# Output projections computed in two turns over the tokens, in a two-block transformer kernel on one Trainium2 core

## The reference, cut to what matters

```python
def rms_norm_2(x, g):
    y = xf * rsqrt(mean(xf * xf, axis=-1) + EPS);  return y * g

# layer i of 2; hx and hc hold 1024 features of 512 and 256 tokens
hx = rms_norm_2(x, g_pre) * (1.0 + scale_x) + shift_x
hc = rms_norm_2(ctx, g_pre) * (1.0 + scale_c) + shift_c
z = h @ w_in                        # queries, latents, gates ...
m = sum over 3 branches of sigmoid(g) * ((y * silu(z)) @ w_branch)
out = m @ w_o                       # the output projection, 1024 x 1024
x   = x   + gate_x * rms_norm_2(out_x, g_post)
ctx = ctx + gate_c * rms_norm_2(out_c, g_post)     # layer 0 only
```

## Time and profile before

| | |
|---|---|
| median of three runs | 2616.11 us |
| the profiled execution's own time | 2613.08 us |
| its span in the profile | 2611.3 us |
| TensorE busy with matmuls | 2467.3 us, 94% |
| VectorE, ScalarE, GpSimd busy | 45%, 35%, 20% |
| mean granted TensorE clock | 0.968 of full |

### The profile page before, as it was taken

How to read it: one execution, slowest core, us unless ns; L and a number is a source line. 1 busy time by engine, 2 the same in 40 slices (tenths; PEclk the granted TensorE clock), 3 DMA queues, 4 the chain that set the end, 5 groups by cost and what they waited for, 6 DMA issues and landing times.

```text
span 2611.3 us, 34190 instructions
## 1 busy us (share of the span) xinstructions
PE 2467.3 (94%) x14039; PEld 1976.7 (76%) x14039; DVE 1180.7 (45%) x1849; ACT 915.4 (35%) x1576; POOL 532.1 (20%) x381
## 2 busy tenths in 40 slices
PE   6887888899999999999999999999989999999998
PEld 5665666677788876778877888888866677878876
DVE  3735545454433444562257313323457633733432
ACT  3324543342222234552246211123335533632223
POOL 3003222140200211231004110012433210321023
PEclk8987899999999989999999999999989999999998
DMA  5231133245443311001210122113121023023232
GB/s 166 65 115 33 33 119 124 74 153 162 142 133 97 109 59 41 25 17 49 81 41 2 49 73 65 57 57 106 50 85 33 25 65 113 9 65 111 75 109 85
DMA packets 195740, 200.60 MB, mean 77 GB/s; under 512 B 15832, under 2 KB 189624, under 8 KB 195330
## 3 DMA queue, kind: packets, MB, share of 16 engines
q1 hardware_dynamic: 191106, 178.23, 21.8%
q10 hardware_dynamic: 4480, 20.19, 2.0%
HBM read 187.92 MB, written 10.49 MB: 76 GB/s over the span
## 4 chain that ended last, share of the span: by engine, by line
PE 85%; DVE 6%; ACT 4%; POOL 2%; issue 2%; DMA 1%; ACTq 0%; POOLq 0%; SPq 0%; DVEq 0%
PE PS L719 20%; PE PS L720 20%; PE PS L722 20%; PE PS L837 5%; PE PS L867 4%; PE PS L851 3%; DVE WL L1888 1%; PE PS L798 1%; ACT WH L1317 1%; PE PS L910 1%; PE PS L937 1%; PE PS L923 1%; PE PS L966 1%; POOL RB L2638 1%; PE PS L775 1%
## 5 line engine op out<-in xcount | busy, mean ns | idle before, releaser
L719 PE MATMUL PS<-HH,WH 128*128 128x512 f32 (+3 forms) x2048 | 757.0, 370 | 9.7 <-DVE WL L1888 4.8
L720 PE MATMUL PS<-HL,WH 128*128 128x512 f32 (+3 forms) x2048 | 726.9, 367 | 0.0
L722 PE MATMUL PS<-HH,WL 128*128 128x512 f32 (+3 forms) x2048 | 659.2, 365 | 0.0
L1888 DVE TENSOR_TENSOR WL<-WB,WH 128x2048 fp32r<-128x2048 f32 (+3 forms) x158 | 324.0, 2051 | 666.4 <-ACT WH L1317 658.5
L719 PEld LDWEIGHTS PS<-HH,WH 128*128 128x128 f32 (+1 forms) x2048 | 384.1, 188 | 117.0 <-issue 13.9
L720 PEld LDWEIGHTS PS<-HL,WH 128*128 128x128 f32 (+1 forms) x2048 | 384.0, 187 | 71.6 <-issue 2.9
L1317 ACT ACTIVATE WH<-WB 128x2048 fp32r<-128x2048 f32 (+3 forms) x158 | 265.1, 1678 | 340.1 <-PE PS L722 270.7
L722 PEld LDWEIGHTS PS<-HH,WL 128*128 128x128 f32 (+1 forms) x2048 | 348.1, 188 | 44.6
L2663 POOL TENSOR_SCALAR SA<-SA,ST 128x768 f32<-128x768 f32 (+4 forms) x80 | 142.0, 1776 | 534.8 <-DVE ST L1969 534.8
L2638 POOL TENSOR_TENSOR RB<-RB,SA 128x512 f32<-128x512 f32 (+2 forms) x65 | 89.3, 1374 | 391.2 <-ACT SA L1336 330.0
L1957 DVE TENSOR_REDUCE ST<-PS 128x1 f32<-128x768 f32 (+4 forms) x176 | 130.0, 739 | 71.0 <-PE PS L837 57.5
(11 more groups left out here) (366 smaller groups left out, 3716.7 us busy)
## 6 DMA issues: line engine op xcount, KB each, us to landing
WB<-in_w_in_dram SPq DMA_DIRECT2D x61, 1024.0 KB, 5.2
WB<-in_w_ff_dram SPq DMA_DIRECT2D x32, 1024.0 KB, 5.4
WB<-in_w_mod_dram SPq DMA_DIRECT2D x24, 1024.0 KB, 5.3
WB<-in_w_branch_dram SPq DMA_DIRECT2D x24, 512.0 KB, 3.5
WB<-in_w_o_dram SPq DMA_DIRECT2D x8, 1024.0 KB, 5.2
WB<-in_w_in_dram SPq DMA_DIRECT2D x14, 512.0 KB, 5.1
XTc<-xd ACTq DMA_DIRECT2D x2, 3072.0 KB, 10.0
WB<-in_cmp_w_dram SPq DMA_DIRECT2D x4, 1024.0 KB, 5.4
```

The source lines that it names most:

```text
L719: pe.matmul(D[0:m, d + o:d + o + w], h, xh[:, o:o + w], start=first, stop=False)
L720: pe.matmul(D[0:m, d + o:d + o + w], h, xl[:, o:o + w], start=False, stop=False)
L722: t = pe.matmul(D[0:m, d + o:d + o + w], lo, xh[:, o:o + w], start=False, stop=last)
L1888: dve.tensor_tensor(b.of(WL[s % NH]), b.of(WB[b.n % NW]), b.of(WH[s % NH]).bitcast(F32), ALU.subtract).then_inc(*done("wl", s))
```

## The change

The projections of both layers are cut by tokens. In layer 0 the first turn is `x` (512 columns) and the second, late turn `ctx` (256); in layer 1 they are the two halves of `x`, 256 columns each. The late turn takes the output tiles in the order 4, 5, 6, 7, 0, 1, 2, 3: the first four find their weights still in `WH` and `WL`, the others need blocks 0 and 1 loaded and split again, two more blocks for each layer. Its eight tiles lie side by side in two PSUM buffers. The sums, the roots, the spread and the making of layer 1's inputs are written once for each side; those of the first turn stand ahead of the late turn's evacuation on ScalarE, VectorE and GpSimd, and between the late turn's tiles on TensorE. `ql1` starts on the `x` half alone; the `ctx` half is made behind `ql1`'s first two tiles, and `kvl1` does its `x` columns before its `ctx` columns. In layer 1 the first half's transposes stand between the late tiles. `XTc`, `OT`, `ot`, `AC` and `QS` get other places in memory.

```diff
--- before.py
+++ after.py
@@ weight_blocks
-        cut(f"o{l}", I["w_o_2"][l])
+        for u in range(6):
+            i = u if u < 4 else u - 4
+            name = f"o{l}" if u < 4 else f"o{l}c"
+            add(Block(name, i, 8, 256, True, lambda w, s=I["w_o_2"][l][:, 256 * i:256 * i + 256]: [
+                (w[:, :, :], s.rearrange("(k p) c -> p k c", p=128))], ("lin", f"o{l}" if u < 2 else f"o{l}c", 2 * i + 1)))
@@ build
+        TURNS = {0: {"x": (0, NX, 0), "c": (NX, NC, 1)}, 1: {"x": (0, 256, 0), "c": (256, 256, 0)}}
+        LATE = (4, 5, 6, 7, 0, 1, 2, 3)
@@ tensor_program: ql1 and kvl1
+                    ps.order = [2, 3]
+                    linear_pair("ql1", hx(NT), nt, queries, lambda k: [next_low("x", k)])
+                    out_sums("c")
+                    tile = linear("ql1", hx(NT), nt, queries, parts=[1], pace=4)
+                    next(tile)
+                    next(tile)
+                    spread_columns("o0c", NC)
+                    spread_columns("h1c", NC)
+                    drain(tile)
+                    linear_sides("kvl1", 2, NT, lambda j: [("kvr_a" if j % 2 else "kvr_d", 1, j)],
+                                 lambda s, k: [next_low("c", k)] if s else [])
@@ tensor_program: the end of a layer
+                def out_sums(side):
+                    o, n, _ = TURNS[0][side]
+                    N, H, Q = f"o0{side}", f"h1{side}", f"oo{side}"
+                    ps.order = [2, 3] if side == "x" else [0, 1]
+                    D = slot(("norm", N), ("on", 0, side, 7))
+                    pe.wait_ge(*at("nadd", N, 7))
+                    add_columns(D, 0, n, RB[rb[N]], True, True).then_inc(*done("nsum", N))
+                    E = slot(("norm", H), ("hn", H, 7))
+                    pe.wait_ge(*at("cross", side, 7, "sum"))
+                    add_columns(E, 6, n, AC[0][:, o:o + n], True, True)
+                    pe.wait_ge(*at("nadd", Q, 7))
+                    add_columns(E, 0, n, AC[1][:, o:o + n], False, True).then_inc(*done("nsum", H))
+                    ps.order = [0, 1] if side == "x" else [2, 3]
+                def between(j):
+                    if l == 0:
+                        if j == 5:
+                            out_sums("x")
+                        elif j == 6:
+                            spread_columns("o0x", NX)
+                            spread_columns("h1x", NX)
+                    elif j == 4:
+                        last_sums("x")
+                    elif j == 5:
+                        spread_columns("o1x", 256)
+                    elif j in (1, 3):
+                        turn_out("x", j // 2)
-                drain(linear(f"o{l}", hx(nt), nt, lambda j: [("ot_a", l, j)], parts=[1, 2, 3]))
+                drain(linear(f"o{l}", half("x"), TURNS[l]["x"][1], lambda j: [("ot_a", l, "x", j)], parts=[1, 2, 3]))
+                for i, j in enumerate(LATE):
+                    b = of[f"o{l}" if i < 4 else f"o{l}c"][j // 2]
+                    if i % 4 == 0:
+                        ps.order = [i // 4]
+                        D = slot(("late", l, i // 4), ("ot_a", l, "c", LATE[i + 3]))
...
+                    t.then_inc(*done("lin", f"o{l}c", j))
+                    between(j)
@@ scalar_program: the end of a layer
+                def early_steps():
+                    if l == 0:
+                        yield
+                        out_roots("x")
+                        late_weights(1)
+                        for f, _ in enumerate(next_high("x")):
+                            if f in (1, 3):
+                                late_weights(f + 2)
+                    else:
+                        root("o1x", 256, 1024)
...
                 for j in range(8):
-                    if j % 2 == 0:
+                    if j % 2 == 0 and j < 6:
                         begin(f"o{l}", j // 2)
+                    out_tile("x", j, j)
                 if l == 0:
+                    drain(early_steps())
+                    begin("ql1")
+                    drain(late_tiles())
+                else:
+                    beside(late_tiles(), early_steps())
```

More of the change, by code:

```diff
@@ L482, in build, with beside @@
         segs = {0: [(0, NX, 0), (NX, NC, 1)], 1: [(0, NX, 0)]}
+        TURNS = {0: {"x": (0, NX, 0), "c": (NX, NC, 1)}, 1: {"x": (0, 256, 0), "c": (256, 256, 0)}}
+        LATE = (4, 5, 6, 7, 0, 1, 2, 3)
+        def beside(late, early):
+            early = iter(early)
+            for _ in late:
+                next(early, None)
+            drain(early)
         nts = (NT, NX)
@@ L693, in loaded, with linear @@
                 return WB[b.n % NW]
-            def linear(name, x, width, freed, ready=None, parts=None, pace=0, after=None, cut=0):
+            def linear(name, x, width, freed, ready=None, parts=None, pace=0, after=None, cut=0, to=None):
                 for b in of[name] if parts is None else [of[name][p] for p in parts]:
@@ new lines, in tensor_program @@
+                ps.order = [0, 1]
+                linear_pair(f"o{l}", half("x"), TURNS[l]["x"][1], lambda j: [("ot_a", l, "x", j)],
+                            lambda k: [("ml_d" if k % 2 else "ml_p", l, k)])
+                drain(linear(f"o{l}", half("x"), TURNS[l]["x"][1], lambda j: [("ot_a", l, "x", j)], parts=[1, 2, 3]))
[4 more added lines that the diff above has]
+                        D = slot(("late", l, i // 4), ("ot_a", l, "c", LATE[i + 3]))
+                    if i % 2 == 0:
+                        wh, wl = whole(b)
+                    to, c = D[:, 256 * (i % 4):256 * (i % 4) + 256], 128 * (j % 2)
+                    for k in range(8):
+                        xh, xl = half("c")(k)
+                        pe.matmul(to, wh[:, k, c:c + 128], xh, start=k == 0, stop=False)
+                        pe.matmul(to, wh[:, k, c:c + 128], xl, start=False, stop=False)
+                        t = pe.matmul(to, wl[:, k, c:c + 128], xh, start=False, stop=k == 7)
+                    t.then_inc(*done("lin", f"o{l}c", j))
+                    between(j)
@@ L1686, in scalar_program @@
                     root("h0x", NX, 1024)
-                for f in range(8):
+                for f in range(8) if l == 0 else ():
                     D = SD[sd["hn", f"h{l}", f]]
@@ L2451, in vector_program @@
                     if j == 2:
+                        if l == 1:
+                            next_sums("c")
                         begin(f"ql{l}", 1)
+                        if l == 1:
+                            inputs = next_inputs("c")
+                            for _ in range(4):
+                                next(inputs)
                     dve.wait_ge(*at("sq", f"qn{l}", j))
```

447 lines of the change are left out of this document (312 added, 135 removed).

## The result

The changed kernel takes 2620.17 us (median of 20 runs, 2617.65 to 2623.94) against 2615.95 for the kernel before, measured beside it (20 runs, 2611.81 to 2620.7): a ratio of 1.0017, 95% interval 1.0011 to 1.0023. Forecast were 2620.0, and "no change that can be told" as the likeliest case. The profiled execution has a span of 2616.1 us, 4.8 over that of before.

What follows compares the result with a forecast made beforehand. The prediction took the kernel as bound by TensorE's matmul time (busy 94%). Layer 1's +6.7 and layer 0's -2.8 gave +3.9 us: span 2615.2, execution 2617.0, plus 3.0 for a median of 2620.0; range 2604 to 2632.

Steps and rivals of the forecast that it cites:

- likeliest case: Whole kernel: no change that can be told, spans of 2613 to 2621 us, chance 0.42.
- wait for GpSimd, for the second block: Layer 0's first turn: TensorE stands 1.5 us at tile 6, then 4.1 us for the second block's weights.
- late turn's wait for its weights: Layer 0's late turn: TensorE waits 2 us for the second `o0c` block before the last two tiles.
- idle ahead of `ql1`; its start: Layer boundary: TensorE idles 7.8 us for VectorE's last next input; `ql1` starts at 1899.0, before at 1900.50.
- `kvl1` and `qn1` done: Start of layer 1: `kvl1` and `qn1`'s sums are done at 1942.0 us, against 1944.8 before.
- Layer 0's gain: Layer 0's late turn through `qn1`'s sums: 2.8 us gained by starting `ql1`'s pair on the `x` half.
- Layer 1's loss: Layer 1's projection to the end: 6.7 us lost, ending at 2618.0 against 2611.3.
- The low clock stays: Sums, spread and idling in layer 0, also layer 1: low clock persists, slower, 2624 to 2630 us; chance 0.25.
- VectorE falls behind: Layer boundary: GpSimd holds up all low parts and the `ctx` sums, slower, 2626 us; chance 0.10.
- The chain keeps up: Layer boundary: VectorE's passes need 29 us instead of 37, no wait before `ql1`, faster, 2610 us; chance 0.15.
- The head stalls are smaller: First turns: no clock losses, layer 1's waits hidden by each other, 6 us less, 2610 us; chance 0.05.
- Narrow matmuls are dearer: Both layers' narrowed matmuls cost more per column, at the dearest 18 us, 2638 us; chance 0.03.

Runs made afterwards that it cites:

- third run: The changed kernel with both spread norms of the x side in the two halves of one PSUM buffer and `ql1`'s pair in another: 2616.48 us.
- first run: The changed kernel with layer 1's projection as before (one turn of 512 columns), leaving only layer 0's part of the change: 2613.63 us.
- second run: The changed kernel with the projection's second weight block split ahead of the pair in both layers: 2616.73 us.
- fourth run: The kernel before, with only the projection's second weight block split ahead in both layers: 2612.71 us.
- eighth run: Changed kernel, layer 1 in one turn, x norms in one PSUM buffer, `ql1`'s third tile before `ctx` sums, second block split ahead (layer 0: ScalarE's half only): 2599.0 us.
- ninth run: The kernel before with the second weight block split ahead in both layers, an unchanged repeat of the same kernel: 2610.11 us.
- later runs: Changed kernel, layer 1 in one turn, x norms in one PSUM buffer, then also `ql1`'s third tile before `ctx` sums, split-ahead variants: 2606.91, 2602.51, 2599.0 us.

## Why the prediction was right

The time (2620.0 forecast, 2620.17 measured) and the likeliest case came true, and most steps did, measured from each kernel's own pair:

| from the pair of layer 0 | forecast | measured |
|---|---|---|
| wait for GpSimd, for the second block | 1.5 and 4.1 | 1.33 and 3.91 |
| `x` sums | 1862.0 + 5.6 - 1809.55 = 58.1 | 58.8 |
| late turn's wait for its weights | 2 | 1.66 |
| idle ahead of `ql1`; its start | 7.8; 89.5 | 7.16; 89.7 |
| `ctx` sums | 104.5 | 104.2 |
| `kvl1` and `qn1` done | 132.5 (before 135.2) | 133.5 |
| layer 1, pair to end (before 68.6) | 2618.0 - 2542.7 = 75.3 | 74.2 |

**Layer 0's gain was mis-sized.** Forecast was 2.8 us gained, with the place where `qn1`'s sums are done as the last one looked at. There 1.8 were indeed gained (133.5 for 135.2). But the sum stopped one tile too early; what comes behind it was put at nothing. Behind it `kr1` takes the PSUM buffer of the second `kvl1` tile, and ScalarE copies that tile out only after the root that hangs on `qn1`'s sums:

```profile
1941.11 0.26 ACT L1832 ACTIVATE QN<-PS,EP 128x4 f32<-128x4 f32 x1 [1.24 <-PE PS L819]
1941.27 0.80 ACT L1828 ACTIVATE KVL<-PS 128x768 f32<-128x768 f32 x1
```

(ScalarE's timeline of the changed kernel). TensorE waits 1.05 us, and the clock, at 0.72 from 1942 to 1948, makes `kr1` 9.9 us long (1942.12 to 1952.06) instead of 8.4. The kernel before has no wait there; in the third run, with another buffer for `kr1`, both are gone. The next sums stand here, first in the kernel before, then in the changed one:

```profile
1953.15 1.39 PE L775 MATMUL PS<-CM,RB 128*128 128x1 f32 x12
```

```profile
1952.06 1.39 PE L819 MATMUL PS<-CM,RB 128*128 128x1 f32 x12
```

From pair to them (1952.06 - 1807.62 = 144.4, before 1953.15 - 1809.55 = 143.6) the gain has turned into 0.8 lost. All this is against one profile of before. By the medians of the first run layer 0's part gains 1.9 us, so how far its whole falls short of the 2.8 stays open; the wait and its 2.7 us, which the third run took away, do not.

**Layer 1's loss was over-sized by 1.1 us**, 0.35 of it up to the last late tile (60.15 us from the pair, forecast 60.5), the rest in the tail behind it (14.05 for 14.8). The mechanism holds: the first turn's half-wide pair does 5.6 us less work inside a time set by GpSimd and VectorE, and the 5.6 us come behind it. The first run shows that loss as a whole, 5.4 us. The forecast took the 1.8 us outside the span as fixed; here they grew by 0.75. Nor does it hang on the wait for the second block: with the split ahead, layer 1 takes 71.4 us in two turns (second run) and 65.1 in one (fourth).

Against the profile of before, from pair to pair I was 3.9 us too hopeful (2.8 gained, 1.1 lost), in layer 1 1.1 too gloomy. That the span is 2616.1 where 2615.2 was forecast, and not 2.8 more, is due to the 1.93 us by which this execution reached the first pair earlier; and the median came true to 0.2 us because it lies 4.1 above the profiled span, not 4.8. So the last microseconds of the agreement are luck.

**The rivals.** "The low clock stays" fell: it was full from 1831 to 1884 and from 1903 to 1914, where `ql1`'s pair ran, and in layer 1 from 2578 to 2603. "VectorE falls behind" fell too: the pair and the `ctx` sums came within 0.3 us of the sum. VectorE's three low parts beside GpSimd took 1.04, 1.35 and 1.32 us where later ones took 0.7, 1.6 us held up in all where 1.5 had been counted. "The chain keeps up" fell by the 7.16 us of idling. "The head stalls are smaller" fell by 1.33, 3.91, 2.99 and 4.32. "Narrow matmuls are dearer" fell: the steps that hold the 256-column matmuls of both layers came out within 1 us of sums made with 0.117 us each.

What the change was good for shows in the eighth run: layer 0 in two turns takes 722.5 us from pair to pair where one turn takes 733.2 (three of four profiles; 737.0 in the other), once the head of the turn, the gate ahead of `ql1` and the order behind it are mended. How much of these 10.7 us needs the two turns is not shown: the split ahead alone gave one turn nothing in layer 0 (ninth run), but a one-turn kernel with another order behind `ql1`'s pair was not tried. In layer 1 no kernel in two turns beat one turn; none with the buffers and order of the later runs was tried there.

## What to carry to other kernels

Cutting a product so that the chain behind it starts early pays only as far as the other engines finish it early; follow their chain to the point where TensorE has next to meet it, and one buffer further. A first turn that is narrower inside a time set by others is work postponed, microsecond for microsecond. And where an engine's idle gap is used for work moved ahead, look at who is busy in that gap: ScalarE's half of a weight split cost nothing there, VectorE's half delayed GpSimd by 2 us.

## What the runs showed of the hardware that was not expected

- VectorE and GpSimd, each with two inputs in SBUF, lengthen each other also for long instructions: 2.29 to 3.29 us, and 3.66 to 5.66 for two. The late tiles' adds, which I had priced at half of a lone residual (0.71 us), took 0.89 us on average on GpSimd beside VectorE's products, the first two of them 0.75.
- Where the clock falls within the same stretch of one-column matmuls differs from execution to execution: at 1878 to 1880 it was 0.50 in the fourth run and 1.00 in the ninth, which are the same kernel and spent 737.03 and 733.34 us between the same two instructions.
- Sums and spreads that lie between 256-column tiles left the clock full for all of 53 us. Before, with 72 one-column matmuls in a row, it was 0.51 from 1882 to 1900, from inside these sums to the end of 5.88 us of idling. Which of the two kept it low there was not separated.
- The first 1800 us, which lie ahead of the change, differed by 5.7 us among the profiled executions, more than the effect that was to be measured. The one kernel that was profiled twice had 1807.60 and 1807.74, so how much of it is the kernel's is open.
- An execution takes longer than its span by 1.8 us in every kernel whose layer 1 has one turn, and by 1.84 to 3.68 in those where it has two.
